# The attention output product of a two-block transformer kernel as one level of Strassen, with its weight sums gathered within layer 2's attention

## The reference

```python
h = rms_norm(x, norm_g)
u = jnp.einsum('bsd,dc->bsc', h, w_in)
v_c, b_c, c_c, z_c, q, k, v, z_a, gate_logits = jnp.split(u, SPLIT_POINTS, axis=-1)
y_c = b_c * causal_depthwise_conv(c_c * v_c, conv_w) * jax.nn.silu(z_c)
y_a = jnp.einsum('bsc,cd->bsd', y_c, w_conv_out)
o = sliding_window_attention(rms(q), rms(k), v, sinks) * jax.nn.silu(z_a)
y_b = jnp.einsum('bsc,cd->bsd', o, w_attn_out)          # the product that is changed
gates = jax.nn.sigmoid(gate_logits + gate_b)
g_a, g_b = jnp.split(gates, N_BRANCHES, axis=-1)
return x + jnp.einsum('bse,ed->bsd', g_a * y_a + g_b * y_b, w_out)
```

## Time and profile before

| | |
|---|---|
| median of three runs | 817.2 us (816.49 to 817.74) |
| the profiled execution | 816.7 us |
| its span | 814.7 us |
| TensorE busy | 808.5 us |
| weight loads of TensorE | 687.1 us |
| VectorE / ScalarE / GpSimd busy | 609.4 / 321.9 / 182.6 us |
| granted TensorE clock | 1.00 |

### The profile page before, as it was taken

The page is one execution under the profiler, slowest core; times in us unless marked ns, Lnnn a source line. Parts: engine busy times, 40 slices in busy tenths (PEclk is TensorE's granted clock), DMA queues, the critical chain, the costliest instruction groups (busy, mean ns, idle before and its releaser), DMA issues.

```text
span 814.7 us, 11429 instructions
## 1 busy us (share of the span) xinstructions
PE 808.5 (99%) x4220; PEld 687.1 (84%) x4220; DVE 609.4 (75%) x1096; ACT 321.9 (40%) x701; POOL 182.6 (22%) x189
## 2 busy tenths in 40 slices
PE   9999999999999999999999999999999999999998
PEld 7778888888888888888888888888888888999986
DVE  4998778768984476885579788978952269599998
ACT  4374465632212255334445554441000122355580
POOL 2212111111111221121324445444323224000000
PEclk9999999999999999999999999999999999999999
DMA  7332214445143222653365555566876335866562
GB/s 239 87 97 77 79 52 153 158 157 179 53 155 126 82 83 77 208 175 90 91 130 130 125 119 120 128 130 155 168 165 158 104 88 145 233 182 183 182 205 78
DMA packets 129565, 108.92 MB, mean 134 GB/s; under 512 B 4525, under 2 KB 101350, under 8 KB 129510
## 3 DMA queue, kind: packets, MB, share of 16 engines
q1 hardware_dynamic: 123142, 95.60, 38.4%
q0 software_dynamic: 6336, 12.58, 9.4%
q10 hardware_dynamic: 32, 0.01, 0.0%
HBM read 106.08 MB, written 27.26 MB: 164 GB/s over the span
## 4 chain that ended last, share of the span: by engine, by line
PE 92%; DVE 5%; issue 1%; ACT 1%; DVEq 0%; ACTq 0%
PE proj L1736 24%; PE proj L1738 24%; PE proj L1737 24%; PE bank_t L1750 3%; PE bank_o L1825 2%; DVE x L1447 1%; DVE w_lo L1142 1%; PE score L1738 1%; PE score L1737 1%; PE score L1736 1%; PE score L1900 1%; PE score L1899 1%; PE score L1811 1%; PE score L1810 1%; PE bank_o L1918 1%
## 5 line engine op out<-in xcount | busy, mean ns | idle before, releaser
L723 POOL TENSOR_SCALAR w_hi<-w_raw 128x1024 fp32r<-128x1024 f32 x109 | 128.8, 1182 | 436.2 <-DMA w_raw<-in_w_in_dram 310.8
L1142 DVE TENSOR_TENSOR w_lo<-w_raw,w_hi 128x1024 fp32r<-128x1024 f32 x145 | 179.9, 1244 | 60.2 <-POOL w_hi L723 59.6
L1736 PE MATMUL proj<-xt_hi,w_hi 128*128 128x512 f32 (+1 forms) x448 | 171.1, 382 | 0.0
L1738 PE MATMUL proj<-xt_hi,w_lo 128*128 128x512 f32 (+1 forms) x448 | 168.1, 375 | 0.0
L1737 PE MATMUL proj<-xt_lo,w_hi 128*128 128x512 f32 (+1 forms) x448 | 167.8, 375 | 0.0
L1738 PEld LDWEIGHTS proj<-xt_hi,w_lo 128*128 128x128 f32 x448 | 84.4, 188 | 15.5
L1737 PEld LDWEIGHTS proj<-xt_lo,w_hi 128*128 128x128 f32 x448 | 84.5, 189 | 14.2
L1736 PEld LDWEIGHTS proj<-xt_hi,w_hi 128*128 128x128 f32 x448 | 84.5, 189 | 13.9
L1736 PE MATMUL proj<-w_hi,xt_hi 128*128 128x512 f32 x152 | 61.0, 401 | 0.2 <-ACT prob L922 0.2
L1738 PE MATMUL proj<-w_hi,xt_lo 128*128 128x512 f32 x152 | 59.5, 392 | 0.0
L1737 PE MATMUL proj<-w_lo,xt_hi 128*128 128x512 f32 x152 | 59.4, 391 | 0.0
(11 more groups left out here) (420 smaller groups left out, 1774.4 us busy)
## 6 DMA issues: line engine op xcount, KB each, us to landing
w_raw<-in_w_in_dram SPq DMA_DIRECT2D x79, 512.0 KB, 3.8
w_sums<-in_w_in_dram SPq DMA_DIRECT2D x8, 1024.0 KB, 7.5
w_raw<-w_sums SPq DMA_DIRECT2D x32, 256.0 KB, 3.3
w_raw<-in_w_out_dram SPq DMA_DIRECT2D x14, 512.0 KB, 3.3
w_raw<-in_w_in_dram SPq DMA_DIRECT2D x26, 256.0 KB, 3.6
w_sums<-w_sums POOLq DMA_DIRECT2D x6, 1024.0 KB, 9.9
w_sums<-in_w_out_dram SPq DMA_DIRECT2D x4, 1024.0 KB, 6.8
w_sums<-in_w_in_dram POOLq DMA_DIRECT2D x4, 1024.0 KB, 9.9
```

The lines of the kernel that those rows point to most:

```text
L723: pool.tensor_scalar(hi, raw, 1.0, 1.0, ALU.mult, ALU.mult).then_inc(hi_done, 1)
L1142: dve.tensor_tensor(lo, raw, hi.bitcast(F32), ALU.subtract).then_inc(w_split, 1)
L1736: pe.matmul(out, left[0], right[0], start=first, stop=False)
L1738: return pe.matmul(out, left[1], right[0], start=False, stop=last)
```

## The change

The attention output product (8 pieces, 128 columns of the weight each) becomes 14 pieces: seven half-block products for each of two column pairs, every one with 24 matmuls of 256 columns. The ordinary pieces become 110, and the convolution output product moves to n = 102 to 109. The left sums of `o` are made by VectorE (`attended_sum`), rounded by ScalarE and given a low part by VectorE (`attended_low`); VectorE combines the products from PSUM into `y_b` (`combine_out`), where ScalarE evacuated them before. The weight sums get a fourth group (`ATTENDED`), gathered first. Sixteen copies are now issued at n = 12 to 27 (layer 1) where twelve were at n = 20 to 27 and 48 to 51; sixteen gathers at n = 53, 54, 56, 57, 59, 60, ... 75 where twelve were at n = 56, 59, 62, ... 89.

```diff
-U_AOUT = U_CONV + KC
-U_COUT = U_AOUT + KC // 4
+U_COUT = U_CONV + KC
 UNITS = U_COUT + KC // 4
-GATES = 4 * UNITS
+AOUT = 4 * U_COUT
+OUT_PIECES = 7 * 2
+COUT = AOUT + OUT_PIECES
+GATES = 4 * UNITS + OUT_PIECES
...
+OUT_ORDER = [A11, A12, A22, S2, S1, S4, S3]
-GROUPS = 3
+GROUPS = 4
+ATTENDED = 3
...
-COPY_AT = [*range(4 * U_GA, 4 * U_O0), *range(4 * U_Z0, 4 * U_Z1)]
-SUM_AT = [4 * U_Z1 + 4 + 3 * i for i in range(4 * GROUPS)]
+COPY_AT = range(4 * U_RQK, 4 * U_O0)
+GROUP_ORDER = [ATTENDED, 0, 1, 2]
+SUM_AT = [4 * U_Z1 + 1 + 3 * i // 2 for i in range(4 * GROUPS)]
...
+                if n == AOUT:
+                    sp.wait_ge(w_gathered[ATTENDED], 16 * 4)
...
             def gather(i):
-                group, step = divmod(i, 4)
+                group, step = GROUP_ORDER[i // 4], i % 4
                 t = (0, 2, 1, 3)[step]
-                if i == 0:
-                    pool.wait_ge(w_copied, 16 * 4 * GROUPS)
+                if step == 0:
+                    pool.wait_ge(w_copied[group], 16 * 4)
...
+            def take_first_out(pair):
+                act.wait_ge(yc_done, KC)
+                if pair:
+                    act.wait_ge(out_combined, COMBINED[S2])
+                act.wait_ge(piece_done, AOUT + 7 * pair + 1)
+                act.activation(u_sum, out_bank(7 * pair), ACT.Copy).then_inc(out_first, 1)
...
+            def combine_out(x):
+                pair, i = divmod(x, 7)
+                product = OUT_ORDER[i]
+                if product in (A11, A22):
+                    return
+                psum, kept = out_bank(x), out_bank(7 * pair + OUT_ORDER.index(A22))
...
+                elif product == S3:
+                    dve.scalar_tensor_tensor(out=out(1, 1), in0=v_sum_out, scalar=-1.0, in1=psum, op0=ALU.mult, op1=ALU.subtract).then_inc(out_combined, 1)
+                    dve.tensor_tensor(w_sum, w_sum, psum, ALU.add).then_inc(out_combined, 1)
+                    dve.wait_ge(out_combined, 7 * pair + 6)
+                    dve.tensor_tensor(out(1, 0), w_sum, kept, ALU.add).then_inc(out_combined, 1)
...
                     elif kind == "OS":
                         dve.wait_ge(o2_gated, WIN_STEPS)
-                        done(dve.tensor_copy(o2_hi[:, m, :], gT2[:, m, :]))
-                        dve.tensor_tensor(o2_lo[:, m, :], gT2[:, m, :], o2_hi[:, m, :].bitcast(F32), ALU.subtract).then_inc(o2_split, 1)
+                        dve.wait_ge(o2_hi_done, m + 1)
+                        tokens = slice(0, 256 if m < 4 else S)
+                        dve.tensor_tensor(o2_lo[:, m, tokens], gT2[:, m, tokens], o2_hi[:, m, tokens].bitcast(F32), ALU.subtract).then_inc(o2_split, 1)
...
+            def attended_product(x):
+                n = AOUT + x
+                product = OUT_ORDER[x % 7]
+                wait_low(n)
...
+                else:
+                    wait_combined_out(x - 8)
+                if x < 7 and LEFT[product][0]:
+                    pe.wait_ge(so_split, (S2, S1, S4, S3).index(product) + 1)
+                left = left_of_attended(product)
+                w = [ring_parts(n, i)[0] for i in (1, 2)]
+                for j in range(2):
+                    for k in range(4):
+                        last = products(out_bank(x)[:, j, :], [t[:, k, j * P:(j + 1) * P] for t in w], [t[:, k, :] for t in left], k == 0, k == 3)
+                last.then_inc(piece_done, 1)
...
                         if u == U_COUT:
                             pe.wait_ge(yc_done, KC)
+                            wait_combined_out(8 + q)
```

More of the change, by code:

```diff
@@ L446, in left_of, with sum_of_attended, left_of_attended @@
             return [t[:, chunk:chunk + 4, token:token + 256] for t in ((hi, lo), (s_hi, s_lo))[source]]
+        def sum_of_attended(product):
+            place = {S2: 0, S1: 1, S4: 2}
+            if product == S3:
+                return [quarter(t, 1, 0) for t in (o2_hi, o2_lo)]
+            return [t[:, 4 * place[product]:4 * place[product] + 4, :] for t in (so_hi, so_lo)]
+        def left_of_attended(product):
+            source, chunk, token = LEFT[product]
+            if source:
+                return sum_of_attended(product)
+            return [t[:, chunk:chunk + 4, token:token + 256] for t in (o2_hi, o2_lo)]
         def pair_of(t, c, r):
@@ L983, in _ @@
                         gate_step(n - GATES)
[L984 to L985 removed]
+                    if (n, half) in SO_HI_AT:
+                        product, after_sums = ((S2, 3), (S1, 1), (S4, 4), (S3, 2))[SO_HI_AT.index((n, half))]
+                        act.wait_ge(so_summed, after_sums)
+                        act.activation(sum_of_attended(product)[0], raw_sum(product), ACT.Copy).then_inc(so_hi_done, 1)
+                    if half == 1 and AOUT <= n < COUT:
+                        if (n - AOUT) % 7 == 0:
+                            take_first_out((n - AOUT) // 7)
+                    if half == 1 and COUT + 2 <= n < COUT + 6:
+                        q = n - COUT - 2
                         act.wait_ge(sx_summed, (4, 6, 8, 10)[q])
@@ L1307, in take_tiles, with attended_sum @@
                                 split_convolved(t)
+            def attended_sum(i):
+                x11, x12, x21, x22 = (quarter(gT2, row, col) for row in range(2) for col in range(2))
+                if i == 0:
+                    dve.wait_ge(o2_split, KC)
+                    dve.tensor_tensor(x22, x22, x21, ALU.subtract).then_inc(so_summed, 1)
+                elif i == 1:
+                    dve.wait_ge(so_summed, 1)
+                    dve.tensor_tensor(x21, x11, x21, ALU.subtract).then_inc(so_summed, 1)
+                elif i == 2:
+                    dve.wait_ge(so_summed, 2)
+                    dve.scalar_tensor_tensor(out=x11, in0=x22, scalar=-1.0, in1=x11, op0=ALU.mult, op1=ALU.subtract).then_inc(so_summed, 1)
+                else:
+                    dve.wait_ge(so_summed, 3)
+                    dve.scalar_tensor_tensor(out=x12, in0=x12, scalar=-1.0, in1=x11, op0=ALU.mult, op1=ALU.subtract).then_inc(so_summed, 1)
@@ L1717, in _ @@
                         take_tiles(n, half)
-                    if half == 1 and WIN_FIRST <= n < 4 * U_AOUT and not splits_wait(n, half):
+                    if half == 1 and WIN_FIRST <= n < AOUT and not splits_wait(n, half):
                         for m in ROUNDED_AT[n]:
                             split_piece(m)
+                    if (n, half) in SO_LOW_AT:
+                        attended_low(SO_LOW_AT.index((n, half)))
+                    if (n, half) in SO_SUM_AT:
+                        attended_sum(SO_SUM_AT.index((n, half)))
                     if (n, half) == (0, 0):
```

157 lines of the change are left out of this document (110 added, 47 removed).

## The result

| | before | changed |
|---|---|---|
| median, runs | 816.78 us, 5 | 834.33 us, 5 (832.54 to 835.63) |
| the profiled execution, its span | 816.7, 814.7 us | 833.03, 831.3 us |

The ratio is 1.021 (95% interval 1.0193 to 1.0226): 17.5 us slower, where 1.9 were predicted and 823.0 was the upper end of the range. The direction held the largest chance.

What follows compares the result with a forecast made beforehand. TensorE's issue rate was taken to bound the kernel. Product - 3.15, gathers + 4.8 and tail + 0.2 gave + 1.85 us, so 819.0 us for the median of the runs, range 814.0 to 823.0.

Steps and rivals of the forecast that it cites:

- The product: Attention output product: 336 shorter matmuls taking 40.35 us replace 192 taking 43.5 us, 3.15 us less.
- I take no wait for it: Output product: load, rounding and low part take 6.5 us of the 8.6 us available, so TensorE never waits.
- rival 3: Output product: slower loads starve the short pieces, 2.1 us on top, 821.1 us; chance 0.05.
- The copies and the tail: Sixteen layer 1 copies cost nothing; last combinations of the output product delay the convolution output product by 0.2 us.
- The gathers: Attention: GpSimd waits for a group's third gather, making selects late for TensorE's value products; 4.8 us, bounds 1.6 to 10.
- the term: Attention: the cost of closer gathers, 3.7 us of late selects plus 0.8 and 0.3 us of loads, 4.8 us.
- Loads behind a gather: Attention: a load waits until a gather in flight is through; 0.8 us for the last group, 0.3 for two between.
- the 2.2 us to spare: Attention, m = 2: selects end at 418.5 us, wanted at 420.7, which swallows the first group's load delay.
- its own upper bound: Attention: the most that the waits from gathers were taken to cost, 10 us.
- rival 2: Attention: the queue fills with gathers and loads, waits reach 10 us, 824.2 us; chance 0.12.
- Rival 1: Attention: waits stay under 1.5 us in all, so the gain is kept, 814.2 up to 815.6 us; chance 0.27.
- Rivals 3 and 4: Short output product pieces starve, 821.1 us, chance 0.05; attention waits only 1.5 to 3.1 us, 815.7 to 817.2, chance 0.12.

Runs made afterwards that it cites:

- E9: The changed kernel with its sixteen gathers three pieces apart from piece 35 to 80 and the left sums earlier: 830.58 us, ratio 1.0161.
- E11: The changed kernel with its gathers two pieces apart from piece 49 to 79 and the left sums earlier: 814.71 us, ratio 0.9961.
- E12: The changed kernel with its gathers two pieces apart from piece 50 to 80 and the left sums earlier: 815.27 us, ratio 0.9965.
- E10: The changed kernel with its gathers three pieces apart from piece 35 to 80, the left sums where the change has them: 831.49 us, ratio 1.0176.
- E6: The kernel before with only its twelve copies moved, all behind pieces 12 to 23 of layer 1: 817.72 us, ratio 1.0003.
- E1: The changed kernel with its sixteen gathers two pieces apart, from piece 53 to 83: 818.39 us, ratio 1.0016.
- E3: The changed kernel with only the fourth gather of each group one piece later, behind the selects: 817.85 us, ratio 1.0004.
- E5: The changed kernel with its gathers two pieces apart from piece 53 and the left sums one piece to one and a half earlier: 816.92 us, ratio 0.999.
- E4: The changed kernel with useless matmuls put ahead of the value products of m = 2, 6, 10 and 14: 828.38 us, ratio 1.015.
- E2: The kernel before with only its twelve gathers moved, as close together as in the changed kernel: 829.82 us, ratio 1.014.

## Why the prediction was wrong, step by step

**The product: right.** 40.35 us were worked out from the gate products' rate. E9, E11 and E12 measured 40.31.

**"I take no wait for it": wrong by 1.9 us.** The chain load, rounding, low part was added up with the durations that each operation has alone. In the changed kernel two of them overlap, GpSimd's rounding and VectorE's operations on 1024 elements, and one or both are slow, VectorE's here:

```profile
627.65 2.06 DVE L1401 TENSOR_TENSOR so_lo<-gT,so_hi 128x1024 fp32r<-128x1024 f32 x1
629.64 2.07 DVE L1213 TENSOR_TENSOR w_lo<-w_raw,w_hi 128x1024 fp32r<-128x1024 f32 x1
```

where the earlier trace rows have 1.22. The total of free time (10.2 us) was enough, but the sums' low parts stand ahead of the ring's in the first six pieces. The Trainium skill ("SBUF — State Buffer", Who interferes with whom), which the prediction weighed for the selects alone, names this pair too. E9 against E10 puts 2.06 us on the place of the sums (40.31 against 42.37). That the slow operations are what makes this place dear is read from the trace and was not tested by itself. It was not the short pieces (rival 3), whose ring is the same in both.

**The copies and the tail: right.** Nothing by the median of E6, for twelve of the sixteen; +0.08 us at the convolution output product where 0.2 was taken.

**The gathers: the mechanism was right, the term mis-sized.** The fourth gather of each group went out 0.3 to 0.4 us after the third had landed, and the selects behind it were late at m = 2, 6, 10 and 14, most at 14. Reckoned were 4.8 us; it was 11.6 (10.3 by the table of waits). E1 and E3 take it away by place alone. The two parts of the term, by the rows:

- From the third gather of a group to the end of the selects 12.9 us were taken; at m = 14 it was 13.5 (546.75 to 560.3), as the gather landed after 9.7 but the four selects took 2.8 us instead of 2.4.
- *Loads behind a gather* were taken at 0.8 + 0.3 us. By the rows of before, moved by the delay up to there, the third gathers went out 3.0, 1.2, 1.0 and 1.6 us late at m = 2, 6, 10 and 14. At m = 14 (546.75, for 533.95 + 11.2) the load of 15.2 us was no surprise: it landed 16.6 us after the issue of the first of the two gathers, where 16.2 + 1.0 were reckoned. Left out was the load behind it, late too (8.9 us). So two roundings stood ahead of the selects of m = 13, the second of 1.70 us, and two of these selects took 2.21 us. At m = 2 (409.68, for 406.61 + 0.1) the prediction said that the delay is swallowed by the 2.2 us to spare; it used them up, and TensorE waited 2.03 more. There the rounding between the first two gathers had itself to wait for a load behind the first, and the next rounding for a load behind the second:

```profile
383.14 1.22 POOL L803 DMA_DIRECT2D w_sums<-in_w_attn_out_dram  x1
394.45 1.05 POOL L775 TENSOR_SCALAR w_hi<-w_raw 128x1024 fp32r<-128x1024 f32 x1 [10.09 <-DMA w_raw<-in_w_in_dram]
395.46 1.04 POOL L803 DMA_DIRECT2D w_sums<-in_w_attn_out_dram  x1
...
406.51 1.06 POOL L775 TENSOR_SCALAR w_hi<-w_raw 128x1024 fp32r<-128x1024 f32 x1 [6.94 <-DMA w_raw<-in_w_in_dram]
```

The Trainium skill ("DMA: Bandwidth & Descriptors", Queues, rings and completion order) says that a DMA engine takes turns among its queues packet by packet. The trace agrees, with 669 packets of one queue for 667 of the other in 8 us. So a load does not stand still behind a gather, as the prediction had it, but moves at an eighth of its own rate (42 for 323 GB/s). That such turns do not shield a load, whose packets are a quarter of the gather's, shows in its 11.6 us behind one gather (E5) and 15.2 between two.

**What was left out: the clock.** The prediction read 1.00 in every stretch and took it for given. It holds only for a TensorE that does not stand still. Behind waits of 1.95, 2.70 and 3.65 us it was at half for 3.4, 3.4 and 6.8 us and cost 6.1 us; behind the first, of 2.03 us, it was not. E4 shows the cause, since the same lateness without standing still costs 5.7 us less. With 10 us of waits, its own upper bound, the prediction would have given 824.2 us (rival 2); the rest, up to 834, is the clock (taken at nothing), the product's 1.9 and 1.6 us by which the waits went beyond 10. The Trainium skill ("TensorE: Matmul & The Clock Gate", What's actually happening) says that the slow clock is the default and activity lifts it: that rule was at hand, and the trace agrees.

**The rivals.** Rival 1 is what E11 reached, with other places for the gathers. Rival 2 had the size of the waits and, with loads that are late behind two gathers, half of the reason. Rivals 3 and 4 fell.

Open is why the clock fell behind 1.95 us (in E2 behind 1.82 and 1.83) and not behind 2.03, and why the first 52 pieces took about 1 us more in the experiments.

## What to carry to other kernels

A DMA that another one waits for on an engine's own queue costs whatever stands behind it on that engine; put at least its landing time (here two pieces, 12 us, for 10 us) between the two. Even a gather that nobody waits for is paid by the next load, and by all that stands in order behind what uses this load; so move large transfers to where the loads have spare time and the engines' order holds nothing urgent, and look for the one load that goes out just behind the last of them. Reckon a wait of TensorE of about 2 us or more at more than its length, and judge a kernel whose runs lie far apart by the trace of a long run.

## What the runs showed of the hardware

- TensorE at full rate fell to the lower clock level (0.50 granted) behind single waits of 1.95, 2.70 and 3.65 us, and in E2 of 1.82, 1.83 and 3.28 us; not behind one of 2.03, nor behind one of 1.55 us in E9. It stayed there for 3.4 or 6.8 us, in which a matmul of 512 columns took 0.43 us instead of 0.23. Once TensorE worked again, the profile showed it busy in all of this time.
- A load of 512 KB, 3.7 us by itself, landed after 11.6 us behind one accumulating transfer of 1 MB from DRAM to DRAM, and after 13.4, 14.3 and 15.2 us beside two in a row, while these took 8.2 to 14.4 us themselves.
- While both were in flight, the two queues moved packets one for one (667 and 669 in 8 us). With 512 B for each packet the load moved 42 GB/s, and loads alone 323 GB/s.
- A rounding on GpSimd and a VectorE operation on 1024 elements of float32 each took up to 2.1 us when they overlapped, for 1.05 and 1.22 alone.
